# Low halves of two neighbouring weight blocks made by one VectorE operation of 2048 elements in the up and gate projection

## The chip, the core and the metric

The kernel runs on one core of one Trainium2 chip. The metric is the device time of one execution in microseconds; lower is better. Engines are named as the profile names them: PE is TensorE (matmuls), PEld its weight loads, DVE VectorE, ACT ScalarE, POOL GpSimd, SP the queue of SyncE, which here issues the loads of the weights.

## What is computed

One layer of a hybrid decoder for 256 prompt tokens and 8 sample tokens (264 columns everywhere), with D = 2048 and a hidden width of 5632. The change touches the up and gate projection of the feed-forward part alone:

```python
gu = _rmsnorm(h, g_ffn) @ w_gate_up
h = h + (jax.nn.silu(gu[..., :D_FF]) * gu[..., D_FF:]) @ w_down
```

All inputs and outputs are float32. The kernel multiplies in float16 and keeps the accuracy by splitting each operand in two halves: `hi` is the operand rounded to float16, `lo` is what is left, again in float16. A product is then the sum of hi·hi, hi·lo and lo·hi.

## The kernel before

**Blocks.** Every weight matrix goes through one pipeline in blocks of 128 partitions x 1024 float32 (512 KB). SP loads a block into one of four slots of `raw` (the DMA, line 440). ACT makes the high half, `hi = f16(1024 * raw)` (`split` of ACT, line 573). DVE makes the low half, `lo = f16(1024 * raw - hi)` (`split` of DVE, line 903). Both halves lie in `hl`, which has eight slots. PE then takes the block.

**What orders it.** Four counting semaphores: `landed` (DMA to ACT), `hi_done` (ACT to DVE), `lo_done` (DVE to PE and to SP), `used` (PE to ACT). SP loads block b when `lo_done` says that block b-4 is through, since the four slots of `raw` go round. ACT splits block b when PE has used block b-8. Each engine works in its own order of instructions, written out by hand; `AHEAD = 4` means that the splits run four blocks ahead of PE.

**The stages.** Input projection, mixer, output projection, per-layer embedding, then the feed-forward part: `S_FFN0` (the first 256 hidden columns), `S_FFN` (21 groups of eight blocks, 256 hidden columns each), `S_DOWN` (4 groups of 22 blocks), then `S_GATE` and the final norm.

**One group of `S_FFN`.** Blocks 0 to 3 hold the gate columns and blocks 4 to 7 the up columns of one group, four k-tiles in each. On PE a gate block is 24 matmuls of 264 columns (lines 2031, 2033, 2034). An up block is 8 matmuls of 264 columns and 28 of 132 columns (lines 2059, 2061): the up part uses a scheme with seven products in place of eight, for which DVE must also make sums of weights (`weight_sums`, lines 1444 and 1449). `sums(0, f)` belong to blocks 4 and 5, `sums(1, f)` to blocks 6 and 7. The last of the seven products of a block waits for the last sum of its pair, `sums(u, 2)`.

**DVE's order in a group** (`ffn_group`, line 1478): low half of block 4; `ff_low` (line 1420, the low half of the last group's hidden activations); blocks 5 and 6; `sums(0, 0)`, `sums(0, 1)`; block 7; `sums(0, 2)`, `sums(1, 0)`, `sums(1, 1)`; `gate_ffn` (line 1386, two operations that take the gate tiles out of PSUM); `sums(1, 2)`; blocks 0 and 1 of the next group; in the first 15 groups `square_e` (lines 1454 and 1456); blocks 2 and 3 of the next group; `up_ffn` (lines 1402 to 1414, which takes the up tiles out of PSUM once ACT has copied the first product, line 836). In the last group "the next group" is the first of `S_DOWN`.

**ACT's order in a group** (line 824): high half of block 4; `ff_high` (line 822, waits for `up_ffn` of the group before); blocks 5, 6 and 7; two sigmoids of the gate tiles (line 832, after PE's block 3); blocks 0 to 3 of the next group; the copy of the first product (line 836, after PE's block 7).

**The way into `S_DOWN`.** After the last group DVE runs `ff_low` once more, then a reciprocal root of the embedding's norm (`rstd_row`, lines 937, 938 and 923 to 925, with a square root on ACT at line 843), a memset (line 1513), and only then the low half of block 4 of `S_DOWN`. Because 22 is no multiple of eight, the slots are padded there: the loads of blocks 0 and 1 of `S_DOWN` wait for blocks 6 and 7 of the last `S_FFN` group, and those of blocks 2 and 3, too, come behind them in SP's order.

Of the kernel before, what the change touches and what calls it, by code (L numbers as in the profile page):

```python
# [7 lines left out]
ALU = mybir.AluOpType  # L8
# [28 lines left out]
AHEAD = 4  # L37

WSCALE = 1024.0
# [93 lines left out]
S_FFN = Stage(S_FFN0, DFF // 256 - 1, 8, by_block=True)  # L133
# [99 lines left out]
def build(nc, io):  # L233
    with ExitStack() as ctx:
        def sb(name, shape, dt=F32):
            return ctx.enter_context(nc.sbuf_tensor(name, shape, dt))

        def sem(name):
            return ctx.enter_context(nc.semaphore(name))


        raw = sb("raw", [P, RAW_SLOTS, BLOCK_KT * COLS])
        hl = sb("hl", [P, 2, HL_SLOTS * BLOCK_KT * COLS], F16)
        hi, lo = (hl[:, n, :].rearrange("p (s c) -> p s c", s=HL_SLOTS) for n in range(2))
# [120 lines left out]
        hi_done, lo_done, used = sem("hi_done"), sem("lo_done"), sem("used")  # L365
# [521 lines left out]
        def _(dve):  # L887
            links = [0]
            stt, ts, tt = nc.vector.scalar_tensor_tensor, nc.vector.tensor_scalar, nc.vector.tensor_tensor
# [10 lines left out]
            def split(st, i, j):  # L900

                dve.wait_ge(hi_done, st.block(i, j) + 1)
                stt(lo[:, st.hl_slot(j), :], raw[:, st.raw_slot(j), :], WSCALE, hi[:, st.hl_slot(j), :],  # L903
                    ALU.mult, ALU.subtract).then_inc(lo_done, 1)
# [370 lines left out]
            for b in range(MIX_END):  # L1275
                st, i, j = MIX_BLOCKS[b]
# [105 lines left out]
            def gate_ffn(st, i, g):  # L1382

                for n in range(2):
                    dve.wait_ge(gate_ready, g * 2 + (SIG_FFN + n + 1))
                    stt(tg32[:, n, :], acc[:, n, 0:TOK], C_FFN, gate_t[:, n, :], ALU.mult, ALU.mult).then_inc(acc_free, 1)  # L1386
# [12 lines left out]
            def up_ffn(i):  # L1399

                dve.wait_ge(p1_ready, i + 1)
                tt(u2, p6, comb[:, 0:HALF_T], ALU.add).then_inc(up_chain, 1)
                dve.wait_ge(up_chain, i * 3 + 1)
                tt(comb[:, HALF_T:3 * HALF_T].rearrange("p (a t) -> p a t", a=2),
                   acc_c[:, HALF_T:3 * HALF_T].rearrange("p (a t) -> p a t", a=2),
                   u2.unsqueeze(1).to_broadcast([P, 2, HALF_T]), ALU.add).then_inc(up_chain, 1)
                dve.wait_ge(up_chain, i * 3 + 2)
                tt(comb[:, 3 * HALF_T:], p5, comb[:, 2 * HALF_T:3 * HALF_T], ALU.add).then_inc(up_chain, 1)
                dve.wait_ge(ff_ready, i + 1)
                tt(a32[:, 0, :], acc_a[:, 0:TOK], comb[:, 0:TOK], ALU.add).then_inc(acc_free, 1)  # L1410
                dve.wait_ge(up_chain, i * 3 + 3)
                tt(a32[:, 1, :], acc_b[:, 0:TOK], comb[:, TOK:], ALU.add).then_inc(acc_free, 1)
                dve.wait_ge(acc_free, S_FFN.tile(i, 4))
                stt(a32[:], a32[:], C_FFN, tg32[:], ALU.mult, ALU.mult).then_inc(ffn_chain, 1)

            def ff_low(i):

                dve.wait_ge(ff_hi_ready, i + 1)
                at = bass.ds(i * 2, 2)
                tt(ff_lo[:, at, :], a32[:], ff_hi[:, at, :], ALU.subtract).then_inc(ff_ready, 1)  # L1420
# [14 lines left out]
            def weight_sums(i, u, f):  # L1435

                s0 = S_FFN.hl_slot(4 + 2 * u) * BLOCK_KT * COLS
                w = hl[:, :, s0:s0 + 2 * BLOCK_KT * COLS].rearrange("p h (q k m c) -> p h q k m c", k=2, m=2, c=P)
                s = s_sum[u]
                n = i * (3 * NPAIRS) + 3 * FAST_PAIRS.index(u)  # L1440
                if f == 0:
                    dve.wait_ge(lo_done, S_FFN.block(i, 5 + 2 * u) + 1)
                    for k, x in enumerate((w[:, :, :, 1, 1], w[:, :, :, 0, 0])):
                        last = tt(s[:, k], w[:, :, :, 0, 1], x, ALU.subtract)
                    last.then_inc(sum_ready, 1)
                    return
                dve.wait_ge(sum_ready, n + f)
                x = w[:, :, :, 0, 0] if f == 1 else w[:, :, :, 1, 0]
                tt(s[:, f + 1], x, s[:, 0 if f == 1 else 2], ALU.subtract).then_inc(sum_ready, 1)
# [25 lines left out]
            for n in range(2):  # L1475
                dve.wait_ge(state_out[n], 16 * PAIRS)

            def ffn_group(i, nxt, i_nxt, between=None):

                def sums(u, f):  # L1480
                    if u in FAST_PAIRS:
                        weight_sums(i, u, f)

                split(S_FFN, i, 4)
                ff_low(i)
                split(S_FFN, i, 5)
                split(S_FFN, i, 6)
                sums(0, 0)
                sums(0, 1)
                split(S_FFN, i, 7)  # L1490
                sums(0, 2)
                sums(1, 0)
                sums(1, 1)
                gate_ffn(S_FFN, i, i + 1)
                sums(1, 2)
                for j in range(AHEAD):
                    split(nxt, i_nxt, j)
                    if between and j == 1:
                        between()
                up_ffn(i)  # L1500

            with dve.Fori(0, KT - 1) as i:
                ffn_group(i, S_FFN, i + 1, lambda: square_e(i + 1))
            with dve.Fori(KT - 1, S_FFN.groups - 1) as i:
                ffn_group(i, S_FFN, i + 1)
            ffn_group(S_FFN.groups - 1, S_DOWN, 0)
            ff_low(S_FFN.groups)

# [19 lines left out]
            def scale_e(i, n):  # L1528

                e = tile_of(e_all, i, n)  # L1530
                tt(e, e, rstd_bc, ALU.mult).then_inc(e_ready, 1)

            with dve.Fori(0, S_DOWN.groups - 1) as i:
# [3 lines left out]
                  between=lambda n: scale_e(last_down, n - 4) if 4 <= n < 8 else None)  # L1537
# [20 lines left out]
            at, n = VEC_AT["g_ple"]  # L1558
# [607 lines left out]
```

## Time and profile before

| | before |
|---|---|
| median of 3 runs | 1192.79 us (1191.83 to 1193.65) |
| the profiled execution | 1194.82 us |
| its span from first to last instruction | 1193.0 us |
| PE busy | 1174.3 us, 98% |
| DVE busy | 917.5 us, 77% |
| ACT busy | 555.3 us, 47% |
| DVE, the splits of line 903 | 414 operations, 495.0 us |
| ACT, the splits of line 573 | 414 operations, 420.5 us |
| granted TensorE clock over the span | 0.995 |

Times inside the trace count from the start of the span. A group of instructions has its busy time, the mean duration of one, and the idle time of its engine just before it with what ended that idle time. Idle time of an engine that is not the bottleneck costs nothing. A busy PE is matmuls in flight; successive matmuls overlap, so that one of 264 columns has a duration of about 0.28 us and the next starts 0.11 us after it.

### The profile page before, as it was taken

The page shows a single profiled execution, that of the slowest core. Times are in us where ns is not written, and L with a number is a line of the kernel's source. Part 1 is how long each engine was busy: PE and PEld are TensorE (multiplying, and loading weights), DVE is VectorE, ACT ScalarE, POOL GpSimd, SP SyncE. Part 2 cuts the span into 40 slices and gives each one's busy share as a digit, 9 for nine tenths or more (in the row PEclk, how much of TensorE's full clock was granted, in tenths as well). Part 3 has the DMA queues.
Part 4 walks back from the last instruction along what each step waited for, and adds up shares of the span by engine and source line. Part 5 has one row for each costly group of instructions (what it writes and reads, how often), then busy time and mean ns, then how long its engine had stood idle before and what let it go on. Part 6 is the DMA issues. An engine that isn't in the chain of part 4 may idle for free.

```text
span 1193.0 us, 29333 instructions
## 1 busy us (share of the span) xinstructions
PE 1174.3 (98%) x11678; PEld 1036.2 (87%) x11678; DVE 917.5 (77%) x1470; ACT 555.3 (47%) x789; POOL 55.4 (5%) x80
## 2 busy tenths in 40 slices
PE   9999999999999999999999999999999999999996
PEld 7888888888888799899999989999888888888885
DVE  6688599678868988998989898888865555555686
ACT  7445645554445644444434444444443434343442
POOL 2122210100000100000000000000000000000000
PEclk9999999999999999999999999999999999999998
DMA  8776776766456566666666666666475656565551
GB/s 257 238 218 184 230 216 180 224 177 206 166 198 198 174 208 196 200 192 206 194 211 210 197 203 188 204 194 210 164 242 194 205 184 206 183 208 193 182 155 73
DMA packets 170571, 234.70 MB, mean 197 GB/s; under 512 B 7987, under 2 KB 108570, under 8 KB 170233
## 3 DMA queue, kind: packets, MB, share of 16 engines
q1 hardware_dynamic: 165040, 220.29, 58.1%
q0 software_dynamic: 3968, 11.89, 3.4%
q10 hardware_dynamic: 1504, 1.70, 0.4%
q8 instruction: 40, 0.66, 0.2%
q14 instruction: 19, 0.15, 0.0%
HBM read 226.89 MB, written 7.43 MB: 196 GB/s over the span
## 4 chain that ended last, share of the span: by engine, by line
PE 87%; DVE 7%; ACT 2%; DMA 2%; issue 1%; ACTq 0%; DVEq 0%
PE acc L1665 15%; PE acc L1667 15%; PE acc L1669 15%; PE acc L2031 13%; PE acc L2034 6%; PE acc L2033 6%; PE acc L2059 3%; PE acc L2061 3%; DVE hl L903 3%; PE wrk L2059 2%; PE wrk L2061 2%; DMA raw<-in_w_in_dram 2%; ACT hl L573 1%; PE wrk L1816 1%; PE wrk L1692 1%
## 5 line engine op out<-in xcount | busy, mean ns | idle before, releaser
L903 DVE SCALAR_TENSOR_TENSOR hl<-raw,hl 128x1024 f16<-128x1024 f32 x414 | 495.0, 1220 | 150.2 <-ACT hl L573 146.9
L573 ACT ACTIVATE hl<-raw 128x1024 f16<-128x1024 f32 x414 | 420.5, 1052 | 214.0 <-PE acc L1669 88.1
L2031 PE MATMUL acc<-nrm,hl 128*128 128x264 f16 x1344 | 276.0, 277 | 2.1 <-DVE tg L1386 2.1
L1665 PE MATMUL acc<-nrm,hl 128*128 128x264 f16 x952 | 263.1, 276 | 1.2 <-ACT gate_t L586 0.8
L1667 PE MATMUL acc<-nrm,hl 128*128 128x264 f16 x952 | 263.1, 276 | 0.0
L1669 PE MATMUL acc<-nrm,hl 128*128 128x264 f16 x952 | 263.1, 276 | 0.0
L1665 PE MATMUL acc<-big,hl 128*128 128x264 f16 x720 | 199.0, 276 | 0.0
L1669 PE MATMUL acc<-big,hl 128*128 128x264 f16 x720 | 199.0, 276 | 0.0
L1667 PE MATMUL acc<-big,hl 128*128 128x264 f16 x720 | 199.0, 276 | 0.0
L2034 PE MATMUL acc<-nrm,hl 128*128 128x264 f16 x672 | 186.5, 278 | 0.0
L2033 PE MATMUL acc<-nrm,hl 128*128 128x264 f16 x672 | 186.5, 278 | 0.0
L2031 PEld LDWEIGHTS acc<-nrm,hl 128*128 128x128 f16 x1344 | 129.0, 98 | 20.4 <-DVE tg L1386 2.4
L1665 PEld LDWEIGHTS acc<-nrm,hl 128*128 128x128 f16 x952 | 93.2, 98 | 15.3 <-issue 1.3
L1669 PEld LDWEIGHTS acc<-nrm,hl 128*128 128x128 f16 x952 | 93.4, 98 | 13.1
L1667 PEld LDWEIGHTS acc<-nrm,hl 128*128 128x128 f16 x952 | 93.4, 98 | 12.9
L1665 PEld LDWEIGHTS acc<-big,hl 128*128 128x128 f16 x720 | 70.4, 98 | 10.9 <-DVE a L1410 0.3
L1667 PEld LDWEIGHTS acc<-big,hl 128*128 128x128 f16 x720 | 70.3, 98 | 10.8
L1669 PEld LDWEIGHTS acc<-big,hl 128*128 128x128 f16 x720 | 70.3, 98 | 10.6
L2034 PEld LDWEIGHTS acc<-nrm,hl 128*128 128x128 f16 x672 | 65.9, 98 | 10.2
L2033 PEld LDWEIGHTS acc<-nrm,hl 128*128 128x128 f16 x672 | 66.0, 98 | 9.9
L1665 PE MATMUL acc<-mix,hl 128*128 128x264 f16 x256 | 70.8, 276 | 1.6 <-DVE hid L1266 1.6
L1669 PE MATMUL acc<-mix,hl 128*128 128x264 f16 x256 | 70.8, 276 | 0.0
(361 smaller groups left out, 1674.4 us busy)
## 6 DMA issues: line engine op xcount, KB each, us to landing
raw<-in_w_gate_up_dram SPq DMA_DIRECT2D x168, 512.0 KB, 4.6
raw<-in_w_down_dram SPq DMA_DIRECT2D x88, 512.0 KB, 4.7
raw<-in_w_in_dram SPq DMA_DIRECT2D x80, 512.0 KB, 4.6
raw<-in_w_out_dram SPq DMA_DIRECT2D x32, 512.0 KB, 4.4
raw<-in_w_ple_gate_dram SPq DMA_DIRECT2D x32, 512.0 KB, 4.8
state<-in_state_hgrn_dram POOLq DMA_DIRECT2D x8, 512.0 KB, 6.2
out_new_hgrn_sample_dram<-state POOLq DMA_DIRECT2D x8, 512.0 KB, 5.0
raw<-in_w_gate_up_dram SPq DMA_DIRECT2D x16, 256.0 KB, 3.3
```

What stands on the lines that cost most here:

```text
L573: nc.scalar.activation(hi[:, st.hl_slot(j), :], raw[:, st.raw_slot(j), :], ACT.Copy, scale=WSCALE).then_inc(hi_done, 1)
L903: stt(lo[:, st.hl_slot(j), :], raw[:, st.raw_slot(j), :], WSCALE, hi[:, st.hl_slot(j), :], ALU.mult, ALU.subtract).then_inc(lo_done, 1)
L1665: mm(out, wh, x_hi[:, kt, :], start=first, stop=False)
L1667: mm(out, wh, x_lo[:, kt, :], start=False, stop=False)
L1669: last = mm(out, wl, x_hi[:, kt, :], start=False, stop=final)
L1692: mm(wrk[:, JOB_BANKS - 1, 0:TOK], idle16[:, 0:P], idle16, start=True, stop=True)
L1816: last = mm(out[:, h * P:(h + 1) * P].rearrange("p (a n k) -> p a n k", a=2, k=size), k_pack[:, h, :], right, start=True, stop=True)
L2031: mm(out, wh, n_hi[:, kt, :], start=jj == 0 and kk == 0, stop=False, skip_group_check=bool(up))
L2033: mm(out, wh, n_lo[:, kt, :], start=False, stop=False, skip_group_check=bool(up))
L2034: last = mm(out, wl, n_hi[:, kt, :], start=False, stop=jj == 3 and kk == 3, skip_group_check=bool(up))
L2059: mm(out, left(0, a), right(1, a), start=begin and a == 0 and out is p1, stop=False, skip_group_check=True)
L2061: last = mm(out, left(1, a), right(0, a), start=False, stop=end and a == 1, skip_group_check=True)
```

## The change

In the 21 groups of `S_FFN`, a new `split_two` makes the low halves of two neighbouring blocks by one operation of 128 x 2048 elements. It waits until both high halves are there and adds 2 to `lo_done` at its end. Block 5 is thereby moved ahead of `ff_low` to block 4, block 6 behind `sums(0, 1)` to block 7, and blocks 0 to 3 of the next group become two pairs with `square_e` between them, as before. ACT, PE and SP have the same instructions as before. The two slots of `raw` and of `hl` lie side by side. 168 operations become 84. Other stages keep their single splits.

```diff
+            def split_two(st, i, j):
+
+                dve.wait_ge(hi_done, st.block(i, j) + 2)
+                at, r = st.hl_slot(j), st.raw_slot(j)
+                stt(lo[:, at:at + 2, :], raw[:, r:r + 2, :], WSCALE, hi[:, at:at + 2, :],
+                    ALU.mult, ALU.subtract).then_inc(lo_done, 2)
+
             def ffn_group(i, nxt, i_nxt, between=None):
 
                 def sums(u, f):
                     if u in FAST_PAIRS:
                         weight_sums(i, u, f)
 
-                split(S_FFN, i, 4)
+                split_two(S_FFN, i, 4)
                 ff_low(i)
-                split(S_FFN, i, 5)
-                split(S_FFN, i, 6)
                 sums(0, 0)
                 sums(0, 1)
-                split(S_FFN, i, 7)
+                split_two(S_FFN, i, 6)
                 sums(0, 2)
                 sums(1, 0)
                 sums(1, 1)
                 gate_ffn(S_FFN, i, i + 1)
                 sums(1, 2)
-                for j in range(AHEAD):
-                    split(nxt, i_nxt, j)
-                    if between and j == 1:
-                        between()
+                split_two(nxt, i_nxt, 0)
+                if between:
+                    between()
+                split_two(nxt, i_nxt, 2)
                 up_ffn(i)
```

## Rows read from the trace of the kernel before

**Rows 1.** The page: busy time, share of the span and instructions of each engine.

```profile
PE 1174.3 (98%) x11678; PEld 1036.2 (87%) x11678; DVE 917.5 (77%) x1470; ACT 555.3 (47%) x789; POOL 55.4 (5%) x80
```

**Rows 2.** Stretch table, `S_FFN`: us, busy by engine, granted clock, DMA share, GB/s.

```profile
424.50:851.20 426.70, 426.70 (x4946) 388.32 (x4943) 376.58 (x537) 190.64 (x246) 0.00 (x0) 1.00 0.64 199
```

**Rows 3.** Chain that ended last (start, us, what): block 4 of two successive groups.

```profile
591.24 0.90 PE acc L2031 x8
612.08 0.90 PE acc L2031 x8
```

**Rows 4.** Timeline of DVE, one group: start, us, line, what, count, idle before.

```profile
584.36 0.70 DVE L1420 TENSOR_TENSOR big<-a,big 128x528 f32 x1
585.05 2.36 DVE L903 SCALAR_TENSOR_TENSOR hl<-raw,hl 128x1024 f16<-128x1024 f32 x2
587.33 1.29 DVE L1444 TENSOR_TENSOR state<-hl 128x1024 f16<-128x1024 f16 x2
...
589.26 1.22 DVE L903 SCALAR_TENSOR_TENSOR hl<-raw,hl 128x1024 f16<-128x1024 f32 x1
590.40 0.69 DVE L1449 TENSOR_TENSOR state<-hl,state 128x1024 f16<-128x1024 f16 x1
591.00 1.29 DVE L1444 TENSOR_TENSOR o_tok<-hl 128x1024 f16<-128x1024 f16 x2
...
594.22 2.35 DVE L903 SCALAR_TENSOR_TENSOR hl<-raw,hl 128x1024 f16<-128x1024 f32 x2
596.49 0.42 DVE L1454 TENSOR_TENSOR xe<-xe 128x264 f32 x1
...
597.50 2.36 DVE L903 SCALAR_TENSOR_TENSOR hl<-raw,hl 128x1024 f16<-128x1024 f32 x2
601.63 0.29 DVE L1402 TENSOR_TENSOR xe<-acc,xe 128x132 f32<-128x132 f32 x1 [1.77 <-ACT xe L836]
...
603.43 0.71 DVE L1414 SCALAR_TENSOR_TENSOR a<-a,tg 128x528 f32<-128x528 f32 x1
```

**Rows 5.** Timeline of ACT, start of the next group.

```profile
604.27 0.64 ACT L822 ACTIVATE big<-a 128x528 f32 x1 [1.41 <-DVE a L1414]
604.82 2.94 ACT L573 ACTIVATE hl<-raw 128x1024 f16<-128x1024 f32 x3
```

**Rows 6.** Timelines of PE and PEld: a group's first matmul; its last product's first weights.

```profile
580.28 0.28 PE L2031 MATMUL acc<-nrm,hl 128*128 128x264 f16 x1
```

```profile
593.30 0.10 PEld L2059 LDWEIGHTS acc<-nrm,state 128*128 128x128 f16 x1
```

**Rows 7.** Line 440, one load by itself: duration ns of the issue, when; us to landing.

```profile
L440 SPq DMA_DIRECT2D raw<-in_w_gate_up_dram x1: 373/373/373, 584.6 to 584.6; - x1
...
DMA to landing us min/median/max: 3.7/3.7/3.7
```

**Rows 8.** The same for three loads that follow each other into `S_DOWN`.

```profile
L440 SPq DMA_DIRECT2D raw<-in_w_down_dram x3: 373/373/373, 840.6 to 841.8; - x3
...
DMA to landing us min/median/max: 4.2/5.0/5.7
```

**Rows 9.** Timelines of DVE and PE from the last group into `S_DOWN`.

```profile
835.05 2.35 DVE L903 SCALAR_TENSOR_TENSOR hl<-raw,hl 128x1024 f16<-128x1024 f32 x2
...
851.71 0.30 DVE L1402 TENSOR_TENSOR xe<-acc,xe 128x132 f32<-128x132 f32 x1 [1.92 <-ACT xe L836]
...
860.12 4.56 DVE L903 SCALAR_TENSOR_TENSOR hl<-raw,hl 128x1024 f16<-128x1024 f32 x4
```

```profile
851.70 0.28 PE L1665 MATMUL acc<-big,hl 128*128 128x264 f16 x1
```

**Rows 10.** PE's two longest idle times in the middle of the kernel.

```profile
305.18 0.27 PE L1665 MATMUL acc<-mix,hl 128*128 128x264 f16 x1 [1.57 <-DVE hid L1266]
```

```profile
411.88 0.29 PE L2031 MATMUL acc<-nrm,hl 128*128 128x264 f16 x1 [2.14 <-DVE tg L1386]
```

**Rows 11.** Stretch table behind the longer of them, columns as in rows 2.

```profile
413.10:416.40 3.30, 3.30 (x18) 2.32 (x17) 3.28 (x4) 2.65 (x3) 0.00 (x0) 0.52 0.65 190
```

## The prediction, made before the changed kernel ran

> **What bounds the kernel now.** I read the page's shares first: PE is busy 98% of the span, DVE 77%, ACT 47% [rows 1]. Those are averages over stages, so I went to the stretch table for the stage that is changed. From the middle of the first `S_FFN` group to the end of the last, 426.70 us, PE is busy for all 426.70 us, at the full granted clock of 1.00 (its upper level, 2.4 GHz), while DVE is busy 376.58 us of them [rows 2]. The chain of waits says the same: it runs through PE alone, and block 4 of successive groups comes at 591.24 and 612.08, a period of 20.84 us [rows 3]. What DVE does faster in this stage is therefore worth nothing by itself. What is to be asked is whether the new grouping makes anything late enough for PE to wait. For that I laid DVE's timeline of one group beside ACT's and PE's [rows 4 to 6], and then looked at the way out of the stage [rows 9].
>
> I count each group from its first matmul on PE: 580.28 for one [rows 6], so 601.12 for the next. In that count the next group's first matmul is at 20.84.
>
> **The change, part by part.**
>
> *The operation itself.* Two single splits in a row take 2.35 to 2.36 us, and the operation behind them starts 2.27 to 2.28 us after the first one's start; one single split takes 1.22 and is followed after 1.14 [rows 4]. So the next instruction starts some 0.08 us before the end of the one in front. One operation of 2048 has no row. From below: the same kind of operation on 528 elements takes 0.71 [rows 4], so 496 more elements cost 0.51 us and 1024 more 1.05, which makes 2.27. From above it is two single ones end to end, 2.44. I take 2.28, near the lower end, since the slope is that of one and the same kind of operation, and 2.20 to the next start; 2.36 to the next start is the bad end. DVE's gain is then 84 x 0.08 = 6.7 us.
>
> The Trainium skill ("VectorE: DVE Perf Modes", section "The TRN2 errata") says that a VectorE operation out of SBUF pays a fixed cost once, so that one large tile beats many small ones, and gives (N + 151) cycles at 0.96 GHz for a two-input float32 operation. By that a merge would save 151 cycles, an estimate of 0.16 us, and 84 merges 13 us of DVE's time. The rows show only half of that exposed, since the next instruction starts before the end of the last one. It would be 0 on the time either way as long as PE sets the pace, but it would make the margin below twice as wide.
>
> *Pair 4, 5.* It waits for the high half of block 5, which ACT makes behind `ff_high`. `ff_high` starts at 604.27, so 3.15 in the count, and block 5's at 604.82, 3.70 [rows 5]. Three of ACT's splits in a row take 2.94, each starting about 0.1 before the end of the last, so one takes 1.05. Its end is at 4.76 and the pair starts at 4.79, while in the kernel before block 4's split starts as soon as `up_ffn` is done, 1.14 before `ff_low` (584.36 [rows 4]), at 2.94. DVE is idle for the difference, 1.85 us. Behind that wait stand all of DVE's instructions: `ff_low`, the sums, everything. Now their starts, with the distances between starts in rows 4: `ff_low` 6.99, `sums(0,0)` 7.69, pair 6, 7 at 9.62 (589.26 - 587.33 = 1.93 later), `sums(0,2)` 11.82, `sums(1,0)` 12.42; from there to the next splits 594.22 - 591.00 = 3.22, so pair 0, 1 of the next group at 15.64, `square_e` 17.84, pair 2, 3 at 18.85 (597.50 - 596.49 = 1.01 later), `up_ffn` 21.05. In the kernel before `up_ffn` starts at 601.63, or 21.35 counted from 580.28, because it waits for PE through ACT, with 1.77 us of idle time in front [rows 4]. So the loop still closes, with **0.30 us** to spare of the 1.77. In the groups without `square_e` it is 1.3 us.
>
> *Who waits for the later pieces.* PE takes block 4 at 10.83 (four blocks of 24 matmuls at 0.113 us each, eight of which take 0.90 [rows 3]) and blocks 5, 6, 7 each 2.5 later; pair 4, 5 is through at 7.07, pair 6, 7 at 11.90 against 15.8. Pair 0, 1 of the next group is through at 17.92 against 20.84. The tight one is `sums(0,2)`: it now stands behind a whole pair and ends at 11.82 + 0.69 = 12.51; PE loads the weights made of it at 593.30, which is 13.02 [rows 6]. Before, it ended at 590.40 + 0.69, which is 10.81 [rows 4]. Margin **0.51 us**, in every group. `ff_low` comes 2.9 us later in the count; it is read only in `S_DOWN`.
>
> *The loads.* `raw` slots come free in pairs, so SP issues in pairs, some 0.2 us after the pair's end (584.6 against 584.44, the end of block 4's split [rows 4, 7]) and 0.6 us apart (three issues from 840.6 to 841.8 [rows 8]). A load alone lands in 3.7 us [rows 7]; of the three in a row they land 4.2, 5.0 and 5.7 us after their own issue, 1.3 us apart [rows 8]. The tightest in a group: pair 6, 7 is through at 11.90, the loads of blocks 2 and 3 of the next group go at 12.1 and 12.7, the second lands at 17.6, ACT's split ends at 18.8. Pair 2, 3 is to start at 18.85. It just fits; up to 0.3 us later it still would not move `up_ffn`. The others have about a microsecond. Cost in the stage: 0, hidden by DVE's 1.77 us of idle time per group; if that cover is gone, it is the first rival.
>
> *The way into `S_DOWN`.* This is where I see a cost. In the last group pair 4, 5 starts at 835.05, where the splits of 5 and 6 start now [rows 9]; then `ff_low` 837.25, the sums, pair 6, 7 at about 839.8, through at 842.1. The first four loads of `S_DOWN` wait for that and go out in one train from 842.25 on. Before, the first went at 837.6 and three at 840.6 to 841.8 [rows 8]. Extending that train by one at 1.3 us, the fourth lands 5.7 + 1.1 + 1.3 = 8.1 us after the first issue, at 850.3. High half of block 3 done at 851.5; pair 2, 3 runs from there to 853.8; `up_ffn` starts at 853.7 instead of 851.71 [rows 9], 2.0 us late. All that follows is one dependent chain on DVE and ACT up to the split of `S_DOWN`'s block 4, which moves from 860.12 [rows 9] to 862.1 and ends at 863.4. PE starts `S_DOWN` at 851.70 [rows 9] and needs block 4 after four blocks of 24 matmuls at 0.113 us, 2.71 each: at 862.5 to 862.6. It waits **0.8 us**. From both sides: a fourth landing 0.6 us earlier or 0.7 later gives 0.2 to 1.5 us. Block 0 itself: second load lands 847.8, high half 848.9, pair through 851.3, 0.4 before PE's need. Would such a stop lower the clock? Behind PE's 1.57 us of idle time at 305.18 the matmuls go on at 0.11 us; behind the 2.14 us before 411.88 the granted clock falls to 0.52 for 3.3 us, its lower level, 1.2 GHz [rows 10, 11]. A stop of 0.8 is on the good side of both.
>
> **The sum.** 0 in the 21 groups, +0.8 us at the entry of `S_DOWN`, given back nowhere, since PE is the pace there too. On the profiled execution's own time that is 1194.82 + 0.8 = 1195.6; this execution is 2.0 us above the median of the runs, so for the median 1192.79 + 0.8 = **1193.6 us**.
>
> **The rivals.** *The loop of DVE becomes longer than PE's 20.84 us (slower).* It decides at 0.30 us more than my sum in a group with `square_e`. Against it: all spacings but that of the pair are rows. For it: four pairs at the bad end, 2.36 to the next start, add 0.64, so the loop is 21.18, 0.34 over. PE then falls back by 0.34 in each of 15 groups at `sums(0,2)`, less the little margin left there: 5 us. With the 0.8 that is 1198.6 us. Chance 0.11.
>
> *A late piece in every group (slower).* If block 7's or block 5's high half, or `sums(0,2)`, comes later than 0.51 us beyond my count, PE stops by the excess in each of 21 groups, 0.2 us being worth 4.2 us: 1197.8. For it: loads now go in twos. Against it: blocks 5 and 7 have about a microsecond. Chance 0.05.
>
> *The stop at `S_DOWN` grows past what the clock bears.* The fourth load late by over 1 us gives a stop of about 1.9 and a lowered clock, which cost half of 3.3 us behind 411.88: 1192.8 + 1.9 + 1.7 = 1196.4. Chance 0.05.
>
> *Nothing moves:* the loads land early enough, PE finds block 4 ready, 1192.8. Chance 0.17.
>
> *Faster.* Only if PE has hidden slack that DVE sets. The stretch shows no idle time and matmuls at an even 0.113 us; I know no place that a faster DVE would shorten. Chance 0.03, about 1190.
>
> **How the numbers follow.** My forecast, 1193.6, has 0.59, with a range of its own from 1192.0 to 1194.9. The measurement of this kernel tells some 0.2% or 2.4 us from no change. Within it lie the forecast, the case of no effect and part (0.02) of the clock case: 0.59 + 0.17 + 0.02 = 0.78. Slower is 0.11 + 0.05 + 0.03 = 0.19: the loop, the late piece, and the rest of the clock case. Faster 0.03. The range starts a little under the case of no effect, at 1191.9, and reaches up to the late piece at 1197.8; it leaves out most of the loop rival and the faster case, some 0.15.
>
> **What would show it.** In the profile after: 84 operations of 128x2048 on line 1482 or near with a mean near 2280 ns; `S_FFN` groups still 20.84 us apart; an idle time of DVE of 1.85 us in front of pair 4, 5, released by ACT's split, and only about 0.3 us in front of `up_ffn` in place of 1.77; loads in pairs; a wait of PE in `S_DOWN`'s block 4 released by DVE's line 903. I am wrong if PE waits inside `S_FFN`, if the pair takes over 2.36 us to the next start, or if `up_ffn` no longer waits for ACT's line 836.

## The result, and the profile after

The changed kernel takes 1196.47 us in the median of 20 executions (1193.23 to 1200.56) against 1192.78 us of before (20 executions, 1190.87 to 1194.0). The ratio is 1.0036, 95% interval 1.0028 to 1.0043; by the medians it is 3.7 us slower. The profiled execution took 1197.92 us, its span is 1196.1 us.

From the page of the kernel after, the shares and the two kinds of split (line, engine, operation, shapes, count, busy us, mean ns, idle time before and its releaser); they answer to [rows 1]:

```profile
PE 1175.6 (98%) x11678; PEld 1036.8 (87%) x11678; DVE 912.5 (76%) x1386; ACT 561.0 (47%) x789; POOL 55.3 (5%) x80
L903 DVE SCALAR_TENSOR_TENSOR hl<-raw,hl 128x1024 f16<-128x1024 f32 x246 | 295.8, 1221 | 147.4 <-ACT hl L573 146.5
L1482 DVE SCALAR_TENSOR_TENSOR hl<-raw,hl 128x2048 f16<-128x2048 f32 x84 | 192.2, 2289 | 46.8 <-ACT hl L573 43.9
```

The operation did what it promised, and a little less: 2.289 us for a pair, DVE's busy time down by 5 us. PE's busy time rose by 1.3 us, and more of the span is idle.

**Inside `S_FFN` nothing was lost.** The chain of waits of after has the same period as [rows 3], 610.83 - 589.99 = 20.84 us:

```profile
589.99 0.90 PE acc L2036 x8
610.83 0.90 PE acc L2036 x8
```

The timeline of DVE of after, the group whose first matmul on PE starts at 579.03, against [rows 4]:

```profile
579.54 0.29 DVE L1402 TENSOR_TENSOR xe<-acc,xe 128x132 f32<-128x132 f32 x1 [0.15 <-ACT xe L836]
...
583.88 2.29 DVE L1482 SCALAR_TENSOR_TENSOR hl<-raw,hl 128x2048 f16<-128x2048 f32 x1 [1.82 <-ACT hl L573]
586.09 0.70 DVE L1420 TENSOR_TENSOR big<-a,big 128x528 f32 x1
...
590.84 0.69 DVE L1449 TENSOR_TENSOR state<-hl,state 128x1024 f16<-128x1024 f16 x1
```

The idle time of DVE has moved. 1.82 us of it now stand in front of pair 4, 5, released by ACT's high half of block 5, and of the 1.77 us in front of `up_ffn` 0.15 are left. Counted from 579.03, pair 4, 5 starts at 4.85, `sums(0,2)` at 11.81. Every piece still comes in time.

**At the entry of `S_DOWN` PE stops.** PE's timeline of after, DVE's and ACT's beside it, and the stretch table behind the stop (columns as in [rows 2]). The first line is the last thing PE does ahead of `S_DOWN`:

```profile
849.95 0.66 PE L2075 MATMUL wrk<-xe,ones 128*128 128x264 f32 x2
850.72 0.28 PE L1670 MATMUL acc<-big,hl 128*128 128x264 f16 x1
...
851.97 0.28 PE L1674 MATMUL acc<-big,hl 128*128 128x264 f16 x1
854.60 0.29 PE L1670 MATMUL acc<-big,hl 128*128 128x264 f16 x1 [2.36 <-DVE a L1410]
```

```profile
848.30 2.29 DVE L1482 SCALAR_TENSOR_TENSOR hl<-raw,hl 128x2048 f16<-128x2048 f32 x1 [3.58 <-ACT hl L573]
850.91 2.29 DVE L1482 SCALAR_TENSOR_TENSOR hl<-raw,hl 128x2048 f16<-128x2048 f32 x1 [0.32 <-ACT hl L573]
853.12 0.29 DVE L1402 TENSOR_TENSOR xe<-acc,xe 128x132 f32<-128x132 f32 x1
...
854.12 0.42 DVE L1410 TENSOR_TENSOR a<-acc,xe 128x264 f32<-128x264 f32 x1
```

```profile
849.75 1.06 ACT L573 ACTIVATE hl<-raw 128x1024 f16<-128x1024 f32 x1 [0.20 <-DMA raw<-in_w_down_dram]
```

```profile
855.40:858.80 3.40, 3.40 (x18) 2.34 (x17) 2.62 (x4) 1.93 (x2) 0.00 (x0) 0.51 0.81 295
```

The same place in the kernel before, PE and then DVE; PE shows no idle time there:

```profile
851.20 0.66 PE L2070 MATMUL wrk<-xe,ones 128*128 128x264 f32 x2
...
853.20 0.29 PE L1665 MATMUL acc<-big,hl 128*128 128x264 f16 x1
```

```profile
852.72 0.42 DVE L1410 TENSOR_TENSOR a<-acc,xe 128x264 f32<-128x264 f32 x1
```

In the kernel after, PE has done two of the four tiles of `S_DOWN`'s first block, 12 matmuls, and stops for 2.36 us ahead of the third. The third tile lies in a PSUM bank that still holds up products of the last `S_FFN` group, and line 1410, in `up_ffn`, is what frees it. `up_ffn` starts at 853.12, right behind the pair of blocks 2 and 3, which itself waited for ACT and so for the loads. Then the granted clock falls to its lower level for 3.4 us, in which PE does half the work: 1.7 us more. The two profiles can be added up. The kernel after had reached `S_FFN` 1.25 us earlier in its profiled execution (its stop there ends at 410.63, against 411.88 [rows 10]), over code that is the same in both. It is still 1.25 us ahead at the last matmul in front of `S_DOWN` (849.95 against 851.20), so the 21 groups cost nothing. From there to the third tile it is 4.65 us, against 2.00 before: 2.65 us more. Of these, 2.36 are the stop, and nearly all of the rest is that PE starts `S_DOWN`'s first tile 0.77 us after that matmul, against 0.50: it waits a little for the pair of blocks 0 and 1, which ends at 850.59. With the 1.7 us of the clock that is 4.35, less the 1.25 it is 3.1, which is what the two spans differ by.

### The profile page after: what moved, and what is told of

It is laid out like the page before. It is cut to its first block, busy times and chain, and to the rows that moved or that the text cites. A ratio compares the mean times of both kernels' runs of the same rounds, so it can differ in the third digit from the quotient of the medians.

```text
span 1196.1 us, 29253 instructions
## 1 busy us (share of the span) xinstructions
PE 1175.6 (98%) x11678; PEld 1036.8 (87%) x11678; DVE 912.5 (76%) x1386; ACT 561.0 (47%) x789; POOL 55.3 (5%) x80
## 4 chain that ended last, share of the span: by engine, by line
PE 85%; DVE 8%; DMA 3%; ACT 2%; issue 2%; SPq 0%; ACTq 0%; DVEq 0%
PE acc L1670 15%; PE acc L1672 15%; PE acc L1674 15%; PE acc L2036 12%; PE acc L2039 6%; PE acc L2038 6%; PE acc L2066 3%; PE acc L2064 3%; DVE hl L903 2%; PE wrk L2066 2%; PE wrk L2064 2%; DMA raw<-in_w_in_dram 1%; ACT hl L573 1%; DMA xe<-in_x_prompt_dram 1%; PE wrk L1821 1%
## 5 line engine op out<-in xcount | busy, mean ns | idle before, releaser
L573 ACT ACTIVATE hl<-raw 128x1024 f16<-128x1024 f32 x414 | 426.1, 1053 | 272.5 <-PE acc L1674 89.7
L903 DVE SCALAR_TENSOR_TENSOR hl<-raw,hl 128x1024 f16<-128x1024 f32 x246 | 295.8, 1221 | 147.4 <-ACT hl L573 146.5
L1482 DVE SCALAR_TENSOR_TENSOR hl<-raw,hl 128x2048 f16<-128x2048 f32 x84 | 192.2, 2289 | 46.8 <-ACT hl L573 43.9
L1670 PE MATMUL acc<-mix,hl 128*128 128x264 f16 x256 | 70.8, 276 | 1.6 <-DVE hid L1266 1.6
```

The costliest lines, as they stand in the source:

```text
L573: nc.scalar.activation(hi[:, st.hl_slot(j), :], raw[:, st.raw_slot(j), :], ACT.Copy, scale=WSCALE).then_inc(hi_done, 1)
L1482: stt(lo[:, at:at + 2, :], raw[:, r:r + 2, :], WSCALE, hi[:, at:at + 2, :], ALU.mult, ALU.subtract).then_inc(lo_done, 2)
L1670: mm(out, wh, x_hi[:, kt, :], start=first, stop=False)
```

## The experiments

Two theories stood against each other. *Entry theory:* all of the loss is the stop at the third tile and the clock behind it. *Stage theory:* waiting for two high halves costs something in the groups in some executions, which would also account for the wider spread. The kernels of one batch ran on one chip beside runs of before.

### Pairs in 20 groups, single splits in the last

```diff
-            ffn_group(S_FFN.groups - 1, S_DOWN, 0)
+            ffn_group_single(S_FFN.groups - 1, S_DOWN, 0)
```

`ffn_group_single` is the function as it was before.

> Pairs in the first 20 groups of S_FFN, the last group as in the kernel before. Entry theory (the whole loss arises where S_FFN passes into S_DOWN: up_ffn of the last group comes 2.4 us late, PE stops 2.36 us at the third tile of S_DOWN's first block, and the lowered clock behind the stop costs 1.7 us more): the loss is gone, within 0.1% of before, about 1192.8, with no idle time of PE at S_DOWN. Stage theory (waiting for two high halves leaves only 0.15 us per group in front of up_ffn, and in some executions PE falls back inside the groups): 1195 to 1197 remains.

Measured: 1192.38 us against 1192.45 of before, ratio 0.9998 (0.9989 to 1.0008). PE does not stop at `S_DOWN`. DVE's timeline of this kernel at that place has `up_ffn` waiting for ACT again, after 80 of 84 pairs are made:

```profile
844.25 3.87 DVE L903 SCALAR_TENSOR_TENSOR hl<-raw,hl 128x1024 f16<-128x1024 f32 x3 [0.29 <-ACT hl L573]
850.24 0.30 DVE L1402 TENSOR_TENSOR xe<-acc,xe 128x132 f32<-128x132 f32 x1 [2.13 <-ACT xe L836]
```

The stage theory falls. The pairs are neither gain nor loss in 20 groups, to within 0.1%.

### Single splits in 20 groups, pairs in the last

```diff
-                ffn_group(i, S_FFN, i + 1, lambda: square_e(i + 1))
+                ffn_group_single(i, S_FFN, i + 1, lambda: square_e(i + 1))
...
-                ffn_group(i, S_FFN, i + 1)
+                ffn_group_single(i, S_FFN, i + 1)
```

> The other half alone: single splits in 20 groups, pairs in the last one. Entry theory: the whole loss is there, 1196 to 1197, with a stop of PE of about 2.4 us in S_DOWN's first block and the granted clock at about 0.5 for 3.4 us behind it. Stage theory: 1192.8 to 1193.5.

Measured: 1196.68 us in 6 executions, ratio 1.0037 (1.0022 to 1.0051). Four pairs of the 84 carry the whole loss. PE's timeline and the stretch table of this kernel:

```profile
853.13 0.40 PE L1694 MATMUL acc<-big,hl 128*128 128x264 f16 x1 [2.55 <-DVE a L1410]
```

```profile
853.20:856.40 3.20, 3.20 (x15) 2.17 (x16) 2.39 (x5) 1.93 (x2) 0.00 (x0) 0.50 1.02 360
```

### up_ffn ahead of the last pair

```diff
-                split_two(nxt, i_nxt, 2)
-                up_ffn(i)
+                if nxt is S_DOWN:
+                    up_ffn(i)
+                    split_two(nxt, i_nxt, 2)
+                else:
+                    split_two(nxt, i_nxt, 2)
+                    up_ffn(i)
```

> Pairs everywhere, but in the last group up_ffn stands in front of the pair of blocks 2 and 3 of S_DOWN instead of behind it. Entry theory by order: up_ffn starts as soon as ACT has copied the first product, PE does not stop at the third tile, and block 2 is still in time: 1192.8 to 1193.3. If it is the late loads themselves that PE waits for (rival), the stop moves to block 0 or 2 and 1195 or more remains.

Measured: 1193.21 us, ratio 1.0005 (0.9996 to 1.0014). PE's timeline has two short stops in place of the long one:

```profile
850.28 0.28 PE L1674 MATMUL acc<-big,hl 128*128 128x264 f16 x1 [0.76 <-DVE hl L1482]
852.00 0.29 PE L1674 MATMUL acc<-big,hl 128*128 128x264 f16 x1 [0.20 <-DVE a L1410]
```

Swapping two calls takes most of the loss away, so it was the order on DVE. Some of the rival is in it too: the 0.76 us are PE's wait for pair 0, 1, which the late train of loads makes late. It is under a microsecond and leaves the clock alone.

### Pairs in all of S_FFN, single splits into S_DOWN

```diff
-                split_two(nxt, i_nxt, 0)
-                if between:
-                    between()
-                split_two(nxt, i_nxt, 2)
+                if nxt is S_DOWN:
+                    for j in range(AHEAD):
+                        split(nxt, i_nxt, j)
+                else:
...
```

> Pairs for all blocks of S_FFN, single splits for the four blocks of S_DOWN made in the last group. The loads of S_DOWN still go out in one train of four from about 841. In the profile after, the high half of block 3 ends at 850.8; a single low half of block 3 would then run 850.8 to 852.0 and up_ffn start at about 852.0, 1.1 us after ACT's copy instead of 2.1. If the late train of loads does most of it: a stop of about 1.2 us, no lowered clock, 1194.0. If the pairing of the two operations alone does it: 1192.8.

Measured: 1193.35 us, ratio 1.0012 (1.0003 to 1.0020). The stop is 1.65 us, with the granted clock at 1.00 behind it:

```profile
851.09 0.29 PE L1674 MATMUL acc<-big,hl 128*128 128x264 f16 x1 [1.65 <-DVE a L1410]
```

```profile
851.10:854.50 3.40, 3.40 (x31) 2.96 (x32) 2.59 (x5) 1.93 (x2) 0.00 (x0) 1.00 0.75 255
```

This kernel differs from the one with single splits in the whole last group in pairs 4, 5 and 6, 7 alone, and that one has no stop. So most of the delay of `up_ffn` comes from these two pairs. The traces show the way: pair 6, 7 ends late, the loads of `S_DOWN` that wait for it leave late and together, and the last high half is late with them (849.75 above, where ACT waited for the load). No run delayed the loads by themselves. The joined operations of blocks 0 to 3 add 0.7 us to the stop, and in these two profiles this 0.7 lies between a stop behind which the clock holds and one behind which it falls.

### The stop by itself, in the kernel before

To price the stop without any pair, the last group of the kernel before gets two or three operations of 528 elements, whose results nobody uses, ahead of `up_ffn`. The two kernels differ only in that number.

```diff
                 dve.wait_ge(p1_ready, i + 1)
+                for _ in range(extra):
+                    link(tt(gate_t[:, 2:4, :], e_all[:, 0:2, :], e_all[:, 0:2, :], ALU.add))
```

> The kernel before, with two extra operations of 528 elements on DVE ahead of up_ffn in the last group only (each waited for, about 0.75 us each), so that up_ffn ends about 1.5 us later. If PE's stop at the third tile follows up_ffn one to one and a stop of 1.5 us leaves the clock alone: 1194.3. If any such stop lowers the clock: 1196. If up_ffn had slack in the kernel before: 1192.8.

> The same with three extra operations, so about 2.2 us late, close to the stop in the kernel after. The step of the clock: a stop of 2.2 us and 1.7 us of lowered clock, 1196.7, which is 2.4 us more than with two for 0.75 us more of delay. Without such a step: 1195.0.

Measured: with two, 1194.33 us, ratio 1.0019 (1.0008 to 1.0031), a stop of 1.48 us, clock 1.00 behind it; with three, 1196.11 us, ratio 1.0030 (1.0019 to 1.0041), a stop of 2.22 us and a clock of 0.50. PE's timelines and the stretch tables of the two kernels, two operations first:

```profile
851.24 0.29 PE L1667 MATMUL acc<-big,hl 128*128 128x264 f16 x1 [1.48 <-DVE a L1412]
851.30:855.00 3.70, 3.70 (x34) 3.22 (x35) 2.89 (x5) 1.93 (x2) 0.00 (x0) 1.00 0.04 11
```

```profile
853.89 0.29 PE L1667 MATMUL acc<-big,hl 128*128 128x264 f16 x1 [2.22 <-DVE a L1412]
854.60:857.90 3.30, 3.30 (x18) 2.28 (x16) 2.52 (x4) 1.93 (x2) 0.00 (x0) 0.50 0.00 0
```

Two things follow. `up_ffn` had no slack in the last group of the kernel before: a delay of some 1.5 us becomes a stop of 1.48. And the loss of the changed kernel can be made without it, by a stop of the same size. In the profiles 0.74 us more of stop brings 3.3 us of lowered clock; in the medians it brings 1.8 us. That the step in the medians is larger than the 0.74 us is likely, but not shown: the two intervals overlap.

### DVE's slack in the groups

One more operation of 528 elements per group, behind `sums(1, 2)`, in the first 20 groups, once in the kernel before and once in the changed one.

```diff
                 sums(1, 2)
+                if nxt is S_FFN:
+                    tt(gate_t[:, 2:4, :], e_all[:, 0:2, :], e_all[:, 0:2, :], ALU.add)
```

> The kernel before with one extra DVE operation of 528 elements (0.62 us to the next start) in each of the first 20 groups. DVE has 1.77 us of idle time per group in front of up_ffn: nothing to be seen, 1192.8.

> The changed kernel with the same extra operation in the same groups. DVE's busy time per group is then still only 0.3 us above that of the kernel before, but only 0.15 us are left in front of up_ffn. My account of the loop (wait for block 5's high half, through up_ffn) gives 0.47 us per group too much, in 15 groups with square_e 7 us, less the 0.5 us that PE has in hand at the last sum: 1202 to 1203. The rival, that DVE's lower busy time is what counts, gives 1196.5 as the changed kernel.

Measured: 1191.59 us in the kernel before, ratio 0.9996 (0.9987 to 1.0005), nothing; 1199.17 us in the changed one (4 executions), ratio 1.0059 (1.0044 to 1.0075). The changed kernel has the shorter busy time on DVE and yet no room for 0.6 us. The timelines of the latter kernel, PE inside a group and then ACT's copy at the end of two successive groups:

```profile
592.45 0.23 PE L2066 MATMUL acc<-nrm,state 128*128 128x132 f16 x1 [0.20 <-DVE state L1449]
```

```profile
579.20 0.28 ACT L836 ACTIVATE xe<-wrk 128x132 f32<-128x132 f32 x1 [2.30 <-PE acc L2068]
600.42 0.28 ACT L836 ACTIVATE xe<-wrk 128x132 f32<-128x132 f32 x1 [2.25 <-PE acc L2068]
```

The period is 21.22 us, 0.38 more than 20.84, and PE waits for the last sum of the first pair, as the first rival said it would. My 1202 to 1203 was too high. I had put the loss at 0.47 in 15 groups; it is 0.38 in 12. The operation behind the extra one starts 0.62 us later, and the slack from start to start is 0.24, not the 0.15 of idle time counted from the end of the operation in front; and the first groups use up the margin at `sums(0,2)`. 12 x 0.38 = 4.6 us. That alone would make 1201; the median is lower. In its profile PE's stop at `S_DOWN` was 2.14 us with the clock at 1.00 behind it, and without the 1.7 us of a lowered clock the account gives 1199.4. No trace shows the stop in the other three executions; the mean granted clock of all four is 0.996 to 0.998, that of the 20 of the changed kernel 0.992 to 0.997.

### The same kind of stop at the other end of the stage

PE's longest idle time in the middle of the kernel before is the 2.14 us ahead of `S_FFN` [rows 10], with a lowered clock behind it [rows 11], released by `gate_ffn` of `S_FFN0`. After what the stop at `S_DOWN` costs, this one looked worth removing.

```diff
-            for f in range(2, 4):
-                token_sums_ffn(f)
+            token_sums_ffn(2)
+            gate_ffn(S_FFN0, 0, 0)
+            token_sums_ffn(3)
             split(S_FFN, 0, 2)
...
+                if j == 4:
+                    pe.wait_ge(t_ready, 8)
...
-            pe.wait_ge(t_ready, 8)
             with pe.Fori(0, S_FFN.groups) as i:
```

The call in `evac_ffn0` is taken out for it.

> No pairs. The same kind of stop at the other end of the stage: before 411.88 PE stops 2.14 us for gate_ffn of S_FFN0, which DVE runs behind all four token sums and a split. Here gate_ffn runs behind the third sum, and PE waits for the sums only ahead of block 4. If PE stops there for DVE's order alone: the stop is gone or under 0.3 us, 2.1 us gained, and up to 1.7 more in the executions in which the clock was lowered behind it: 1189 to 1190.5. If something else is late next (low halves of block 2 or 3, up tiles): a stop inside the first group and under 1 us of gain.

> The same mended entry with pairs in the first 20 groups and single splits in the last one. If pairs are neither gain nor loss once the last group is left alone: equal to the kernel with the mended entry and no pairs, 1189 to 1190.5. If DVE's slack of 0.15 us per group costs PE something in some executions: 1191 or more.

> The same mended entry with pairs everywhere and up_ffn ahead of the pair of blocks 2 and 3 in the last group. The stop of 0.76 us at S_DOWN's first block, seen with this order, stays: 0.8 us above the two others, 1190 to 1191.5.

Measured, against 1192.58 of before in this batch: without pairs 1189.18 us, ratio 0.9970 (0.9960 to 0.9981); with pairs in the first 20 groups 1189.84, ratio 0.9981 (0.9972 to 0.9989); with pairs everywhere and `up_ffn` first 1190.63, ratio 0.9986 (0.9977 to 0.9995). In all three PE no longer stops at the entry of `S_FFN`. DVE's timeline of the first, where `gate_ffn` is done by 408.75 and PE goes straight on:

```profile
406.74 1.32 DVE L1432 TENSOR_TENSOR mix<-mix,nrm 128x1056 f16<-128x1056 f16 x2
407.98 0.77 DVE L1386 SCALAR_TENSOR_TENSOR tg<-acc,gate_t 128x264 f32<-128x264 f32 x2
408.66 1.32 DVE L1432 TENSOR_TENSOR mix<-nrm,mix 128x1056 f16<-128x1056 f16 x2
```

The version without pairs beats both kernels of this study, by 3.4 us against before in its own batch, and by some 7 against after, which ran in another batch. Pairs add nothing to it; in the first 20 groups they cost between nothing and 0.2% (the two intervals overlap slightly), which I can't resolve.

## Why the prediction was right where it was, and where it was not

- *PE sets the pace in `S_FFN`, and a faster DVE is worth nothing there:* right. Period 20.84 us in both, and 80 pairs with a ratio of 0.9998.
- *The operation:* 2.289 us against 2.28, next start 2.21 after it (583.88 to 586.09) against 2.20. The joined splits gave 5.0 us less busy time on DVE in the two profiles; 84 x 0.07 is 5.9. The Trainium skill's (N + 151) cycles at 0.96 GHz ("VectorE: DVE Perf Modes", section "The TRN2 errata") are 2.291 us for 2048 elements, and this trace agrees with its 2.289. The 151 cycles per merge that it would save do not all appear, since the next operation already starts before the end of the last.
- *Where DVE's time stands in a group:* right to within 0.1 us. `sums(0,2)` at 11.81 against 11.82, pair 4, 5 at 4.85 against 4.79, its wait 1.82 against 1.85. In front of `up_ffn` 0.15 us were left against 0.30: 0.06 came from a semaphore behind `square_e`, the rest is that I counted from start to start and the row from the end of the operation before.
- *Loads in twos:* they land 3.6 to 3.7 and 4.4 to 4.5 us after their issue in the groups, where I took 3.7 and 5.0. No loss, as said.
- *The way into `S_DOWN`:* a delay of `up_ffn` was rightly seen, but too small, and its price was wrong. I had `up_ffn` 2.0 us late. Counted from PE's last matmul ahead of `S_DOWN` it starts at 3.17 us, against 0.51 before: 2.66 late. The fourth load was slower than my extension of the train, landing 6.9 us after its own issue and 8.6 after the first one's, where I had 8.1. **The step that failed is "all that follows is one dependent chain up to the split of block 4".** I followed `up_ffn` forward on DVE and ACT, and did not ask who waits for `up_ffn` itself. That is PE, 1.36 us into `S_DOWN`, for the PSUM bank that line 1410 frees. In the kernel before there was nothing to spare: PE starts `S_DOWN` at 851.70 and its third tile is due at 853.06; line 1410, which I did not put among my rows, ends at 853.14, and PE takes the tile at 853.20. With no slack, the 2.66 us became a stop of 2.36 (PE was itself 0.27 late) in place of 0.8, and block 4, held up by the same delay, had its own wait covered by it.
- *The clock:* that a stop of 1.57 us leaves the clock alone and one near 2.1 can lower it [rows 10, 11] held in every profile, though the latter does not always do it (last section). The rival with a stop of 1.9 and 1.7 of lowered clock gave 1196.4; measured 1196.47. Its chance, 0.05, was far too low, because I had hung it on late loads in front of block 4 alone. That the two numbers agree to 0.1 us is in part luck: with the 2.65 us measured, the same sum is 1197.1.
- *The direction:* my forecast of 1193.6 was no more than 0.2% from no change, and the result is 0.28 to 0.43% slower; I had given slower 0.19. The result lies inside my range of 1191.9 to 1197.8, but that is luck too: I had taken the upper end from a late piece in every group, which did not occur.

## What to carry to other kernels

When an instruction is moved, list every semaphore that it raises and find each waiter in the next stage too, not only on the engine that it runs on: the first group and the last of a loop have other neighbours, and here 4 of 84 operations made all of the loss. Joining two operations on an engine that is not the bound can cost more of its slack than its busy time gives back, because the joined one starts at the later of two inputs and ends at the later of two outputs: 5 us less busy time, and 1.6 of 1.8 us of slack per group gone to a new place. Stops of the bounding engine at a change of stage are worth looking for, even short ones, because of what can hang on them.

## What the runs showed of the hardware that I had not expected

The same stop lowers the clock in one execution and not in the next. The 2.14 us ahead of `S_FFN` are in the profiles of before, of after and of the eight experiments that leave it in; behind it the granted clock is lowered in four of these ten profiles and stays at 1.00 in six. Its length does not tell them apart: it is 2.13 us in one profile with the lowered clock and 2.15 in two with the clock at 1.00. Stretch tables just behind that stop, first of the kernel after, then of the changed kernel with the extra operation:

```profile
411.30:414.90 3.60, 3.60 (x20) 2.46 (x19) 2.94 (x4) 2.47 (x3) 0.00 (x0) 0.54 0.57 170
```

```profile
410.60:414.60 4.00, 4.00 (x37) 3.47 (x37) 3.31 (x5) 2.14 (x3) 0.00 (x0) 1.00 0.53 145
```

At `S_DOWN` stops of 2.22, 2.36 and 2.55 us came with a lowered clock, one of 2.14 without, and 1.48, 1.65 and the 1.57 of the mixer never with one. Each lowering lasted 3.4 us, so it costs 1.7 us. That can be a part of why executions of one and the same kernel differ by a few microseconds here: the 20 of the changed kernel, with two such stops each, spread over 7.3 us, and their mean granted clock is 0.997 in the fastest and 0.992 in the slowest. It is not all of it. Of the three kernels with neither stop, the 7 executions without pairs spread over 1.1 us, but the 12 with pairs in the first 20 groups over 5.9 (11 of them within 1.7) and the 11 with pairs everywhere over 4.4. What makes these differ was not looked into.
